# Operand sums in SBUF in order of use, weight high parts first, three bank pairs in the down projection

## The reference

```
def half_swiglu(x, g, w_gate, w_up, w_down):
    h = rmsnorm(x, g)
    return x + 0.5 * ((jax.nn.silu(h @ w_gate) * (h @ w_up)) @ w_down)
```

## Time and profile before

| | us |
|---|---|
| median of 3 runs | 1766.95 (1766.27 to 1767.21) |
| the profiled execution | 1768.82 |
| its span | 1767.0 |
| TensorE busy | 1696.9 |
| VectorE busy | 941.4 |
| ScalarE busy | 737.6 |
| GpSimd busy | 698.1 |
| first matmul of FFN 1's ring | 78.97 |
| first matmul of FFN 2's ring | 1401.5 |

### The profile page before, as it was taken

How to read it: one execution, slowest core, us unless ns; L and a number is a source line. 1 busy time by engine, 2 the same in 40 slices (tenths; PEclk the granted TensorE clock), 3 DMA queues, 4 the chain that set the end, 5 groups by cost and what they waited for, 6 DMA issues and landing times.

```text
span 1767.0 us, 41483 instructions
## 1 busy us (share of the span) xinstructions
PE 1696.9 (96%) x16580; PEld 1614.2 (91%) x16580; DVE 941.4 (53%) x1483; ACT 737.6 (42%) x1227; POOL 698.1 (40%) x912
## 2 busy tenths in 40 slices
PE   6799999999799999999999999999999699999998
PEld 6799999999799999898788989898999699999998
DVE  6736537366854545454474453626455744637363
ACT  4444536355523333332243443435234453536442
POOL 3564645554422222121132322324255463645543
PEclk9899999999899999999899999999999899999999
DMA  4352433423432334232054454446353352343522
GB/s 171 126 184 75 140 132 119 155 73 130 150 119 97 103 111 143 93 100 70 31 208 183 169 183 157 180 147 232 137 204 119 131 171 107 115 138 116 188 67 98
DMA packets 57497, 237.29 MB, mean 134 GB/s; under 512 B 7521, under 2 KB 8161, under 8 KB 55905
## 3 DMA queue, kind: packets, MB, share of 16 engines
q1 hardware_dynamic: 49440, 218.35, 34.8%
q10 hardware_dynamic: 7872, 16.37, 2.5%
...
## 4 chain that ended last, share of the span: by engine, by line
PE 81%; issue 6%; DVE 6%; POOL 3%; ACT 2%; DVEq 1%; DMA 0%; ACTq 0%; POOLq 0%
PE ps L394 27%; PE ps L824 23%; PE ps L834 14%; PE ps L1401 3%; POOL w_lo L381 3%; PE ps L2339 1%; PE ps L2516 1%; ACT w_hi L374 1%; PE ps L2453 1%; PE ps L2439 1%; PE ps L2383 1%; PE ps L2459 0%; PE ps L2423 0%; PE ps L1366 0%; PE ps L1521 0%
## 5 line engine op out<-in xcount | busy, mean ns | idle before, releaser
L381 POOL TENSOR_TENSOR w_lo<-w_raw,w_hi 128x256 fp32r<-128x256 f32 x384 | 320.1, 864 | 714.8 <-ACT w_hi L374 714.8
L394 PE MATMUL ps<-h_hi,w_hi 128*128 128x288 f32 x1248 | 295.2, 319 | 35.5 <-POOL w_lo L381 31.5
L394 PE MATMUL ps<-h_hi,w_lo 128*128 128x288 f32 x1248 | 270.5, 299 | 0.0
L394 PE MATMUL ps<-h_lo,w_hi 128*128 128x288 f32 x1248 | 270.4, 299 | 0.0
L394 PEld LDWEIGHTS ps<-h_hi,w_hi 128*128 128x128 f32 x1248 | 204.9, 193 | 57.6 <-POOL w_lo L381 33.1
L394 PEld LDWEIGHTS ps<-h_lo,w_hi 128*128 128x128 f32 x1248 | 204.8, 192 | 0.0
L394 PEld LDWEIGHTS ps<-h_hi,w_lo 128*128 128x128 f32 x1248 | 204.1, 192 | 0.0
L807 POOL TENSOR_TENSOR ring_lo<-raw,ring_hi 128x256 fp32r<-128x256 f32 (+1 forms) x194 | 140.5, 749 | 119.7 <-ACT ring_hi L788 118.9
L374 ACT ACTIVATE w_hi<-w_raw 128x1024 fp32r<-128x1024 f32 x96 | 101.7, 1059 | 110.7 <-PE ps L394 93.7
L1209 DVE SCALAR_TENSOR_TENSOR x<-ps,x 128x576 f32<-128x576 f32 x64 | 48.5, 758 | 145.5 <-PE ps L834 144.4
L807 POOL TENSOR_TENSOR ring_lo<-w_raw,ring_hi 128x256 fp32r<-128x256 f32 (+1 forms) x123 | 88.3, 743 | 79.9 <-ACT ring_hi L788 79.7
...
## 6 DMA issues: line engine op xcount, KB each, us to landing
w_raw<-in_w SPq DMA_DIRECT2D x122, 512.0 KB, 3.4
raw<-in_w SPq DMA_DIRECT2D x48, 512.0 KB, 4.8
...
```

The lines of the kernel that those rows point to most:

```text
L381: last = nc.gpsimd.tensor_tensor(w_lo[par_][:, c], w_raw[par_][:, c], w_hi[par_][:, c].bitcast(F32), ALU.subtract)
L394: last = nc.tensor.matmul(ps[:, b + c, 0:HC], w[par_][:, wk], a[:, k, c * HC:(c + 1) * HC], start=(first and k == 0), stop=(end and k == n ...
```

## The change

The operand sums move from PSUM to SBUF: T1 and T4 in TA, T2 in TB, which lie where g_hi and g_lo have their tiles 4 and 5. The operands are made in the order in which the products use them, B11, T1, B21, T2, T3, T4, B22, and are counted by a semaphore of their own; A12's product now waits for B21's low part only, and the products behind it each for their own operand. T4's high part takes the place of hn_a, so ScalarE waits for T3's low part ahead of it. On ScalarE `split_hi` of the next unit stands ahead of g_high(0) and of the operands. In FFN 2 T3's low part, T4 and B22 are finished behind chunk11. The copy of P2 and chunk11 of the first ring tile are taken out of the loop and stand ahead of blocks 4 to 6 and of the sum S3. hn_b moves to the place of raw buffers 4 and 5, whose first load now waits for B22's low part. The down projection uses three bank pairs in turn, the third being that of the last tile: the first half of D(2) stands right behind S4 and waits for silu and chunk12 of the last tile, and D(u) from 3 on waits for the addition of D(u - 3).

```diff
-OPERANDS = ("B21", "B22", "B11", "T1", "T3", "T2", "T4")
-HN_READY = {"B21": 4, "B22": 4, "B11": 8}
-T_MADE = {"T1": 1, "T3": 2, "T2": 3, "T4": 4}
+OPERANDS = ("B11", "T1", "B21", "T2", "T3", "T4", "B22")
+OPERAND_MADE = {"B11": 4, "T1": 5, "B21": 9, "B22": 9, "T3": 10, "T2": 11, "T4": 12}
...
         with ExitStack() as c:
+            with ExitStack() as c1:
+                sb(c1, "beside_ta", [128, 4, NT])
+                TA = sb(c1, "ta", [128, 4, HC])
+                sb(c1, "beside_tb", [128, 4, NT])
+                TB = sb(c1, "tb", [128, 4, HC])
             g_hi, g_lo = sb(c, "g_hi", [128, PARTS[0], NT], F32R), sb(c, "g_lo", [128, PARTS[0], NT], F32R)
             sg, gt = sb(c, "sg", [128, NT]), [sb(c, "gt%d" % i, [128, NT]) for i in range(2)]
             u2, u3 = sb(c, "u2", [128, HC]), sb(c, "u3", [128, HC])
             raws = [w_raw[0], w_raw[1]] + [sb(c, "raw%d" % i, [128, W8]) for i in (2, 3)]
-            with ExitStack() as c1:
-                HNb = sb(c1, "hn_b", [128, 4, NT])
-            raws += [sb(c, "raw%d" % i, [128, W8]) for i in (4, 5)]
             S3 = sb(c, "s3", [128, 512])
             with ExitStack() as c1:
+                raws += [sb(c1, "raw%d" % i, [128, W8]) for i in (4, 5)]
+            HNb = sb(c, "hn_b", [128, 4, NT])
+            with ExitStack() as c1:
...
-        TPS = ps[:, 4:8, 0:HC]
         a_raw = {"B21": HNb[:, :, 0:HC], "B22": HNb[:, :, HC:NT], "B11": HNa[:, :, 0:HC], "T3": HNa[:, :, HC:NT],
-                 "T1": TPS, "T2": TPS, "T4": TPS}
+                 "T1": TA[:, :, :], "T2": TB[:, :, :], "T4": TA[:, :, :]}
...
-                out += [("D", p, 0, 1), ("D", p, 1, 1)] + [("D", p, u, h) for u in range(2, KD) for h in range(2)]
+                out += [("D", p, 2, 0), ("D", p, 0, 1), ("D", p, 1, 1), ("D", p, 2, 1)]
+                out += [("D", p, u, h) for u in range(3, KD) for h in range(2)]
...
         def down_bank(f, p, u):
-            return 4 if u % 2 else 2 - set_of(f, last_tile(f, p))
+            z = set_of(f, last_tile(f, p))
+            return (2 - z, 4, z)[u % 3]
...
                     pe.wait_ge(evac[0], P0 + n_cl)
-                    pe.wait_ge(sem("dve_lo"), operand_lo_count(f) + 3)
+                    operand_wait(pe, f, "B11")
                 p1(T)
                 if p:
                     x_wait(pe, f, p - 1, 7)
                 else:
-                    pe.wait_ge(sem("dve_lo"), operand_lo_count(f) + 7)
+                    operand_wait(pe, f, "B21")
                 p2(T)
                 p5(T)
...
                     chunk_wait(pe, f, "c11", v)
+                    if v == n_cl:
+                        operand_wait(pe, f, "T2")
...
                 K, KH = PARTS[p], down_half(p)
+                pe.wait_ge(sem("silu_done"), base + FIRST[p] + K)
+                chunk_wait(pe, f, "c12", FIRST[p] + K - 1)
+                block_ready(pe, f, ("D", p, 2, 0))
+                for k in range(KH):
+                    last = down_slice(f, p, 2, k)
+                last.then_inc(sem("blk_used"), 1)
                 pe.wait_ge(sem("g_ready"), base + FIRST[p] + K - 1)
                 for u in range(2):
                     block_ready(pe, f, ("D", p, u, 1))
@@ -925,26 +941,28 @@
                 for u in range(2):
                     down_slice(f, p, u, K - 1).then_inc(sem("blk_used"), 1)
                 for u in range(2, KD):
-                    x_wait(pe, f, p, u - 2)
-                    for h in range(2):
+                    for h in range(u == 2, 2):
                         block_ready(pe, f, ("D", p, u, h))
+                        if u > 2 and h == 0:
+                            x_wait(pe, f, p, u - 3)
                         for k in range(KH * h, KH * h + KH):
                             last = down_slice(f, p, u, k)
                         last.then_inc(sem("blk_used"), 1)
...
+            act.wait_ge(sem("dve_made"), operand_count(f) + OPERAND_MADE[a])
+            if a == "T4":
+                operand_wait(act, f, "T3")
...
             if f == 0:
                 silu(0)
+                split_hi(act, P0 + 2, 0, W8)
                 g_high(act, f, 0)
-                operand_hi(act, f, "B21")
-                operand_hi(act, f, "B22")
-                split_hi(act, P0 + 2, 0, W8)
+                split_hi(act, P0 + 2, 1, W8)
                 silu(1)
                 operand_hi(act, f, "B11")
-                split_hi(act, P0 + 2, 1, W8)
+                operand_hi(act, f, "T1")
                 g_high(act, f, 1)
-                operand_hi(act, f, "T1")
-                operand_hi(act, f, "T3")
                 split_hi(act, P0 + 3, 0, W8)
+                operand_hi(act, f, "B21")
                 silu(2)
                 split_hi(act, P0 + 3, 1, W8)
                 g_high(act, f, 2)
                 operand_hi(act, f, "T2")
-                operand_hi(act, f, "T4")
+                operand_hi(act, f, "T3")
                 block_hi(act, f, 0)
                 block_hi(act, f, 1)
                 silu(3)
+                operand_hi(act, f, "T4")
+                operand_hi(act, f, "B22")
             else:
                 split_hi(act, P0 + 1, 0, W8)
                 silu(0)
-                operand_hi(act, f, "B21")
-                operand_hi(act, f, "B22")
                 split_hi(act, P0 + 1, 1, W8)
                 g_high(act, f, 0)
                 operand_hi(act, f, "B11")
+                split_hi(act, P0 + 2, 0, W8)
                 operand_hi(act, f, "T1")
-                operand_hi(act, f, "T3")
-                split_hi(act, P0 + 2, 0, W8)
                 silu(1)
+                operand_hi(act, f, "B21")
                 split_hi(act, P0 + 2, 1, W8)
                 g_high(act, f, 1)
-                operand_hi(act, f, "T2")
                 block_hi(act, f, 0)
                 block_hi(act, f, 1)
                 silu(2)
-                operand_hi(act, f, "T4")
+                operand_hi(act, f, "T2")
+                operand_hi(act, f, "T3")
             block_hi(act, f, 2)
             block_hi(act, f, 3)
+            chunk_p2(n_cl)
+            block_hi(act, f, 4)
+            if f == 1:
+                operand_hi(act, f, "T4")
+            block_hi(act, f, 5)
             g_high(act, f, n_cl - 1)
-            for i in range(4, 7):
-                block_hi(act, f, i)
+            block_hi(act, f, 6)
+            if f == 1:
+                operand_hi(act, f, "B22")
 
...
-                elif b[0] == "A12":
+                elif b[0] == "A12" and b[1] > n_cl:
                     chunk_p2(b[1])
...
-                    ins = V.tensor_tensor(TPS, HNa[:, :, HC:NT], HNa[:, :, 0:HC], ALU.subtract)
+                    ins = V.tensor_tensor(TA[:, :, :], HNa[:, :, HC:NT], HNa[:, :, 0:HC], ALU.subtract)
                 elif a == "T3":
                     ins = V.tensor_tensor(HNa[:, :, HC:NT], HNb[:, :, HC:NT], HNa[:, :, HC:NT], ALU.subtract)
                 elif a == "T2":
-                    ins = V.tensor_tensor(TPS, HNb[:, :, HC:NT], TPS, ALU.subtract)
+                    ins = V.tensor_tensor(TB[:, :, :], HNb[:, :, HC:NT], TA[:, :, :], ALU.subtract)
                 else:
-                    ins = V.tensor_tensor(TPS, HNb[:, :, 0:HC], TPS, ALU.subtract)
+                    ins = V.tensor_tensor(TA[:, :, :], HNb[:, :, 0:HC], TB[:, :, :], ALU.subtract)
...
@@ -1126,72 +1150,82 @@
                 dve.drain()
                 V.scalar_tensor_tensor(gt[0][:, :], gt[0][:, :], back(0), nry[:, :], ALU.mult, ALU.mult)
                 dve.drain()
-                made(0)
+                multiplied(0)
+                g_low(0)
                 root_copied()
-                for k in range(4, KD):
-                    normalized(k)
+                normalized(0)
+                normalized(1)
                 evac_gate(1)
-                for k in range(4):
-                    normalized(k)
+                normalized(2)
+                normalized(3)
+                combined("T1")
                 evac_up(1)
-                made(1)
-                combined("T1")
-                combined("T3")
-                operand_lo(dve, f, "B21")
-                operand_lo(dve, f, "B22")
+                multiplied(1)
+                normalized(4)
+                normalized(5)
+                g_low(1)
+                normalized(6)
+                normalized(7)
                 evac_gate(2)
                 operand_lo(dve, f, "B11")
                 operand_lo(dve, f, "T1")
+                combined("T3")
+                evac_up(2)
+                multiplied(2)
+                operand_lo(dve, f, "B21")
+                g_low(2)
                 combined("T2")
-                evac_up(2)
-                made(2)
+                combined("T4")
+                operand_lo(dve, f, "T2")
+                evac_gate(3)
                 operand_lo(dve, f, "T3")
-                operand_lo(dve, f, "T2")
-                combined("T4")
                 operand_lo(dve, f, "T4")
```

(49 more changed lines are left out.)

44 lines of the change are left out of this document (21 added, 23 removed).

## The result

The changed kernel takes 1753.26 us (median of 4 runs, 1752.32 to 1755.28), the kernel before 1766.82 on the same chip (1766.27 to 1767.21); the ratio is 0.9922, 95% interval 0.9906 to 0.9938. The gain is 13.56 us, where the prediction has 13.5. The profiled execution has a time of 1752.32 and a span of 1750.5 us, 16.5 shorter than before: 3 us more than the medians, and that excess has to be found too.

A forecast was written before the change was run, and what follows sets the result against it. TensorE, 96% busy, bounds the kernel, so only its empty or half-clock time can be gained. 8.7 + 6.0 - 1.2 = 13.5 us off the 1766.95 median gives 1753.4 us, range 1748 to 1758.5, chance 0.66.

The forecast's parts named there:

- FFN 1's term: Start of FFN 1, new order: 17.3 us of waits and slow restarts gone, 8.6 new; gain 8.7 us.
- part 3: Down projection seams, three bank pairs: 5.9 us new chunk12 waits, less 1.7 and 3.0 saved; loss 1.2 us.
- FFN 2's term: Start of FFN 2, new order: 16.3 us of waits and restarts gone, 10.3 new; gain 6.0 us.
- Part 1: New order of both FFN starts (weight high parts first, operands by use, early P2 copy): gains 8.7 and 6.0 us.
- The gone side: FFN 1's start: TensorE waits of 7.72 and 5.23 us vanish with slow restarts of 2.2 and 2.1; 17.3 us.
- The new side: FFN 1's start: new waits 0.2, 0.3, 5.0 before S1, restart 2.1, 1.0 before S3; 8.6 us.
- Part 2: Operand sums in SBUF: two of ten newly SBUF-fed operations meet a GpSimd split, 0.7 us, already in VectorE's sharing.
- Rival (b): Shared ports at operand sums: all ten SBUF-fed operations wait a whole 0.82 split, 8.2 us: 1760.9 us; chance 0.14.
- (a): Both FFN starts: new waits don't come as VectorE is quicker; 17.3 + 16.3 gone, less 1.2: 1734.6 us; chance 0.06.
- (c): End of operands: VectorE and ScalarE lock step, S3's product no earlier: 1767, or 1768.2 with part 3; chance 0.07.
- (d): Eight down projection seams: granted clock falls at the chunk12 waits, 2.2 us each, 17.6: 1771.0 us; chance 0.07.
- the signs asked for: TensorE's trace: no w_lo waits in units; about 5 us before S1, 6 to 8 before S3; eight seam idles about 0.6.

The follow-up runs named there:

- Experiment 6: Changed kernel with VectorE making B22's low part twice at the end of each FFN's operand chain; 1759.72 us, ratio 0.9955.
- 7: Changed kernel with ScalarE's first-tile u2 copy moved ahead of blocks 7 to 9 and, in FFN 2, B22's high part; 1753.41 us, ratio 0.9919.

## Why the prediction was right

**Size and sign.** 13.5 was forecast, 13.56 measured by the medians, 13.9 by the account of matmuls. That the sum hit so closely is partly luck: FFN 1's term was 1.3 us too high, part 3's loss 1.3 us too high, FFN 2's term 0.4 too low, and the first two cancel.

**Part 1, FFN 1: 8.7 forecast, 7.4 measured.** The gone side held: the waits of 7.72 and 5.23 and their restarts are absent. The new side was 8.6 and came to 0.85 + 1.34 + 3.84 + 0.78 + 2.7 = 9.5. Mis-sized terms: the wait for evac_gate(1), 0.2 against 0.85 (VectorE began it at 42.70, not 42.3); the wait of A11's product for its low part, 0.3 against 1.34; the restart, 2.1 against 2.7; the wait ahead of S1, 5.0 against 3.84, mostly because TensorE arrived later, by 0.65 and by 1.04 from the first two, with VectorE 0.7 late itself. (These terms give 17.3 - 9.5 = 7.8; the last 0.4 to the 7.4 of the account is not assigned.) A11's wait ends with four splits of GpSimd:

```profile
68.10 3.94 POOL L809 TENSOR_TENSOR w_lo<-w_raw,w_hi 128x256 fp32r<-128x256 f32 x4 [5.36 <-ACT w_hi L790]
...
68.80 1.84 POOL L809 TENSOR_TENSOR w_lo<-w_raw,w_hi 128x256 fp32r<-128x256 f32 x1
```

They are blocks 0 and 1, whose high parts ScalarE makes behind those of T2 and T3. The second took 1.84 us instead of 0.73, beside T3's low part (68.64 to 70.05, out of hn_a). T3 read SBUF in the kernel before as well, so these 1.1 us came with the new order, which put the two side by side just ahead of A11, and not with the new place of the sums.

**Part 1, FFN 2: 6.0 forecast, 6.4 measured.** New were 1.30 + 0.25 + 6.93 + 1.6 = 10.1 against 10.3. The chain behind the wait was named rightly, as VectorE's part of it in after shows: T3 low, S3's sum, a product, T4 low, g_low and B22 low from the chunk11 on, then S4's sum, for which ScalarE waits before it can copy u2:

```profile
1386.50 0.46 DVE L1144 TENSOR_TENSOR gt<-gt,ps 128x288 f32<-128x288 f32 x1 [0.16 <-issue]
...
1393.41 1.60 DVE L965 TENSOR_TENSOR B_lo<-hn_b,B_hi 128x1152 fp32r<-128x1152 f32 x1 [0.20 <-ACT B_hi L960]
1395.10 0.70 DVE L772 TENSOR_TENSOR ps<-w_raw,ps 128x512 f32<-128x512 f32 x1
...
1395.89 0.60 ACT L790 ACTIVATE ring_hi<-ps 128x512 fp32r<-128x512 f32 x1 [1.75 <-DVE ps L772]
1396.92 0.60 ACT L790 ACTIVATE ring_hi<-ps 128x512 fp32r<-128x512 f32 x1 [0.43 <-DVE ps L763]
1397.60 0.41 ACT L1050 ACTIVATE u<-ps 128x288 f32<-128x288 f32 x1
```

From chunk11's start to u2 that is 11.1 us, in the text 96.1 to 107.1, 11.0. Experiment 6 bears it out, and so does 7, where the wait moved on instead of going. No wait in the list of after is put down to the late load of up(5), as taken; its landing was not tried by itself.

**Part 2: 0.7 forecast.** In the new order it can be read from VectorE's operations. Of the ten newly fed from SBUF five meet a split, not two: T4's low part takes 1.91 us in FFN 1 instead of 1.36, and in FFN 2 T2's sum takes 1.57, T4's sum 1.72 and T2's low part 1.73, while beside T4's low part it is the split that waits. That is 0.55 + 0.94 = 1.5 us of VectorE's two chains, inside the waits of part 1, and three of GpSimd's splits in FFN 2 grow from 0.73 to 1.86 or 1.92. In the old order it was 0.8 and 0.5 us of TensorE's waits. The step that failed is "GpSimd has 1 to 3 us to spare there, and it costs nothing unless that goes": in the old order it did go, and TensorE waited 1.03 us for it. By the rule of the Trainium skill that the prediction quotes ("SBUF — State Buffer", section "SBUF: two separate sides"), whichever of the two starts first has the shared ports for its whole instruction and the other is blocked. The trace agrees: a split ends some 0.60 us after the VectorE operation that it waited for, whether that took 1.36 or 1.72, and stays at 0.73 beside one that reads PSUM. The prediction held 0.36 against the rule because it is less than a split, but 0.36 is what was left of a split already running, and the most seen is 0.55. The 3.29 us that it took for four undisturbed splits has one of 1.24 in it, beside g_low; undisturbed they take 2.85. Rival (b) falls because five of ten meet, and because each pays the rest of a split and not 0.82.

**Part 3: loss of 1.2 forecast, gain of 0.1 measured.** The direction was wrong here, by less than the medians can tell. The seams cost 0.83 each and not 0.74, 6.7 in all. The third bank pair saves 0.33 ahead of D(2), not 0.2: 2.6 in eight parts, not 1.7. That the weight load runs ahead of its matmul did not shorten the saving below the 0.29 of idle time seen. The g_lo waits give 1.78 in each part of four tiles, with the slow pair behind them, and 0.10 in each part of six, which the prediction did not have: 4.2, not 3.0. Left is 2.6 + 4.2 - 6.7 = 0.1.

**The rivals.** (a), no new waits: false, they came, with 15.3 us of idle time. (c), lock step: false. (d), the clock falls at the seams: false at all eight. Of the signs asked for, all came, one smaller than asked: no wait for w_lo in the units, one wait ahead of S1 (3.84 for "about 5") and one ahead of S3, both with the clock at half behind them, eight idle times of 0.59, none ahead of D(3).

**What stays open.** The medians of after and before differ by 13.6, their profiles by 16.5. The table puts 2.2 of the difference between the FFNs, in work that is the same. Why the clock falls there at other places from execution to execution was not tried. Nor was the new order of the operands tried without the weights' and P2's moves.
